# Moving one block's row gather behind the activation's turn in a routed expert loop

## The reference, cut to what matters

```python
def expert_block(args):
    xb, e = args
    return clamped_swiglu(xb @ w1[e] + b1[e]) @ w2[e] + b2[e]
yb = lax.map(expert_block, (xs, block_exp)).reshape(P, D)
y = jnp.zeros((T, D), h.dtype).at[row_tok].add(yb * row_gate[:, None])
```

## Time and profile before

| | us |
|---|---|
| time, median of 3 runs | 2306.31 (2303.6 to 2308.85) |
| span of the profiled execution | 2306.2 |
| TensorE busy | 2209.2 (96% of the span) |
| VectorE busy | 1194.8 (52%) |
| ScalarE busy | 650.0 (28%) |
| issues of weight chunks (BIG<-in_w, 1 MB each) | 384 |

### The profile page before, as it was taken

The page is one execution under the profiler, slowest core; times in us unless marked ns, Lnnn a source line. Parts: engine busy times, 40 slices in busy tenths (PEclk is TensorE's granted clock), DMA queues, the critical chain, the costliest instruction groups (busy, mean ns, idle before and its releaser), DMA issues. The chain is left out here.

```text
span 2306.2 us, 29645 instructions
## 1 busy us (share of the span) xinstructions
PE 2209.2 (96%) x10363; PEld 1188.4 (52%) x10364; DVE 1194.8 (52%) x2716; ACT 650.0 (28%) x1658; POOL 101.8 (4%) x234
## 2 busy tenths in 40 slices
PE   8999899999999999999999899999999999999997
PEld 3546685478744578777878633333333323333332
DVE  4989468453895563636745453334343333334334
ACT  3018442443221363336333321111111111111112
POOL 0001000000000051002001000000000000000000
PEclk9999999999999999999999999999999999999999
DMA  9670035301477103331241599989989998998998
GB/s 398 250 291 34 1 146 191 110 1 45 175 266 278 39 2 110 110 110 38 74 147 37 231 373 421 421 357 421 422 365 422 421 421 366 421 421 366 421 421 335
DMA packets 110280, 569.68 MB, mean 247 GB/s; under 512 B 11857, under 2 KB 13649, under 8 KB 51441
## 3 DMA queue, kind: packets, MB, share of 16 engines
q1 hardware_dynamic: 110192, 568.54, 61.6%
HBM read 567.46 MB, written 1.05 MB: 247 GB/s over the span
## 5 line engine op out<-in xcount | busy, mean ns | idle before, releaser
L3060 PE MATMUL PS<-BIG,PW 128*64 128x512 f32 x2304 | 514.1, 594 | 15.3 <-DMA BIG<-in_w 14.7
L3060 PEld LDWEIGHTS PS<-BIG,PW 128*64 128x64 f32 x2304 | 161.6, 137 | 353.6 <-issue 301.9
L3312 DVE TENSOR_SCALAR PW<-PS 128x512 f32<-128x512 f32 x36 | 24.9, 692 | 494.6 <-PE PS L3060 494.6
L3108 PE MATMUL PS<-BIG,PW 128*64 128x512 f32 x1152 | 255.4, 595 | 8.6 <-ACT PW L2923 8.6
L386 DVE SCALAR_TENSOR_TENSOR BIG<-BIG,COND_ROWS 128x1024 f32<-128x1024 f32 x128 | 153.4, 1221 | 24.9 <-DMA BIG<-in_w_ada_columns 24.6
L3108 PEld LDWEIGHTS PS<-BIG,PW 128*64 128x64 f32 x1152 | 79.2, 137 | 161.0 <-issue 142.7
L2900 ACT COPY BIG<-PS 128x512 f32<-128x512 f32 x37 | 21.7, 586 | 486.6 <-PE PS L3032 486.6
L1148 PE MATMUL PS<-HT,BIG 128*128 128x512 f32 (+1 forms) x448 | 152.0, 501 | 0.0
L1148 PEld LDWEIGHTS PS<-HT,BIG 128*128 128x128 f32 x448 | 85.1, 190 | 65.3 <-issue 60.3
L658 PE MATMUL PS<-HT,BIG 128*128 128x256 f32 x512 | 111.6, 379 | 1.4 <-PEq L863 1.4
L1553 PE MATMUL PS<-BIG,HT 128*128 128x512 f32 x256 | 110.0, 592 | 0.0
(11 more groups left out here) (547 smaller groups left out, 3171.6 us busy)
## 6 DMA issues: line engine op xcount, KB each, us to landing
BIG<-in_w SPq DMA_DIRECT2D x384, 1024.0 KB, 16.1
BIG<-in_l_w_ada_columns SPq DMA_DIRECT2D x40, 1024.0 KB, 7.2
BIG<-in_l_w_in SPq DMA_DIRECT2D x19, 2048.0 KB, 8.5
BIG<-in_w_ada_columns SPq DMA_DIRECT2D x24, 1024.0 KB, 7.1
BIG<-in_l_w_out SPq DMA_DIRECT2D x8, 2048.0 KB, 8.5
BIG<-in_w_in SPq DMA_DIRECT2D x7, 2048.0 KB, 8.1
BIG<-in_l_w_ada SPq DMA_DIRECT2D x4, 2048.0 KB, 17.9
BIG<-in_w_out SPq DMA_DIRECT2D x2, 2048.0 KB, 7.8
```

The lines of the kernel that those rows point to most:

```text
L3060: ins = nc.tensor.matmul(PS[64 * g:64 * g + 64, 4 + half, :], xt[:, c % 4, c // 4, :], W[:, c, half * F + g * 512:half * F + g * 512 + 512 ...
L3108: ins = nc.tensor.matmul(PS[64 * g:64 * g + 64, 7, :], at_[:, k % 4, k // 4, :], W[:, 8 + k // 2, k % 2 * D + g * 512:k % 2 * D + g * 512 ...
```

## The change

The gather of the rows of block i+1 goes from the middle of `first_products(i)` to `second_products(i)`, right behind the four turns of the activation. The turns of the gathered rows go from before the second products to behind the second of the eight pairs of second products (k == 2, so between chunk 8 and chunk 9). Block 0 keeps its old order (`gather_here=False`). On ScalarE the copy of the turned activation comes ahead of the copy of the gathered rows. The instructions themselves are the same ones, and as many. The diff, cut to its core:

```diff
                     def copies(i):
                         act.wait_ge(loop["act_turned"], i + 1)
                         nc.scalar.copy(at_, PS[:, 7, :].rearrange("p (j g s) -> p j g s", j=4, g=2)).then_inc(loop["act_copied"], 1)
-                        copy_turned(i + 1)
...
                     with act.Fori(1, n) as i:
-                        copy_gathered(i + 1)
                         sigmoid(i)
                         copies(i)
+                        copy_gathered(i + 1)
+                        copy_turned(i + 1)
...
-                    def products_and_gather(i, load):
-                        def gather_between(c):
-                            if c == 3:
-                                gather_next(i)
-
-                        first_products(i, load, beside=gather_between)
...
-                    def second_products(i, load, beside=None):
+                    def second_products(i, load, beside=None, gather_here=True):
                         pe.wait_ge(loop["act_ready"], i + 1)
...
                         ins.then_inc(loop["act_turned"], 1)
-                        turn_gathered(i + 1)
+                        if gather_here:
+                            gather_next(i)
+                        else:
+                            turn_gathered(i + 1)
                         pe.wait_ge(loop["act_copied"], i + 1)
                         for k in range(KT):
+                            if gather_here and k == 2:
+                                turn_gathered(i + 1)
...
-                        products_and_gather(i, load)
+                        first_products(i, load)
                         scatter_last(i)
                         second_products(i, load)
```

More of the change, by code:

```diff
@@ L2931, in _ @@
                     copies(0)
+                    copy_turned(1)
                     with act.Fori(1, n) as i:
-                        copy_gathered(i + 1)
                         sigmoid(i)
                         copies(i)
+                        copy_gathered(i + 1)
+                        copy_turned(i + 1)
                     def square_half(bank):
@@ L3146, in spread_gates @@
                         spread_places(1)
-                    second_products(0, 0, beside=spread_gates)
+                    second_products(0, 0, beside=spread_gates, gather_here=False)
                     load = pe.value_load(plan[0:1, 1:2], min_val=0, max_val=E - 1)
-                    products_and_gather(1, load)
+                    first_products(1, load)
                     scatter_last(1)
@@ L3155, in _ @@
                     load = pe.value_load(plan[0:1, 2:3], min_val=0, max_val=E - 1)
-                    products_and_gather(2, load)
+                    first_products(2, load)
                     pe.wait_ge(loop["bias2_scaled"], 1)
```

## The result

The changed kernel takes 2314.7 us (median of five runs, 2313.2 to 2315.8), the kernel before 2307.9 us beside it. The medians differ by 6.8 us. The ratio is 1.0035, 95% interval 1.0022 to 1.0047: by it the change is slower by 8.1 us, between 5.1 and 10.8. The forecast was 2314.3 us and +8.0.

What follows compares the result with a forecast made beforehand. The prediction took weight transfers and TensorE's five legs after chunk 7 to bound the kernel in turn. Each leg: +1.71 - 0.84 + 0.73 = +1.60 us; five add 8.0, giving 2314.3 us, range 2309.5 to 2319.5.

Steps and rivals of the forecast that it cites:

- The bound: Experts' stage: weight transfers (29.8 us a one-load block) are slower than TensorE's 26.07 us block; both limits take turns.
- the relay: Experts' stage: span 2306.2 us splits into 1505.1 ahead, 57.9 TensorE legs, 720.3 transfers and 22.9 ending.
- the legs: TensorE's path from chunk 7 to the next issue, 14.47 us four times, plus the ending; each forecast +1.60 us.
- the first stretch: Transfers ahead of the first of five waits for chunk 7: counted 0, up to 0.5 us gain kept for the range.
- The gather leaves the first products: Between chunks 3 and 4: removing its 1.71 us only lengthens TensorE's wait at chunk 7, worth 0.
- the steady block: TensorE's regular block from turn to turn, 26.07 us; forecast to fall by 0.11 us, spent waiting at chunk 7.
- The turns between chunks 8 and 9: Gathered rows' four transposes within the second products: +0.73 us on a leg, ScalarE's copy hidden with 1.1 us to spare.
- The sum: Per leg +1.71 - 0.84 + 0.73 = +1.60 us; five legs +8.0 us, median 2314.3 us.
- the transfers' stretches: From an issue to the next chunk 7, four times, 720.30 us together; forecast unchanged within some tenths.
- TensorE isn't the bound: Denies the rival that TensorE bounds the stage and the copy's stall counts: 2297.2 or 2302.5 us, chance 0.08.
- the gather isn't hidden on any leg: Denies the rival that the gather on the leg is hidden: time as before, 2306.3 us, chance 0.13.
- ScalarE's copy isn't late: Denies the rival that the gathered rows' copy is late at k == 2: 0.63 us a block, 2320.2 us, chance 0.07.

Runs made afterwards that it cites:

- the same kernel with a wait of 0.4: Kernel before with scatter moved behind chunk 3, gather behind chunk 7, and ScalarE's sigmoid ahead of the gathered rows' copy: 2310.2 us, ratio 1.0008.
- the kernel that waited 0.82 us a block: Kernel before with only the gather moved from behind chunk 3 to behind chunk 7, ScalarE's order as before: 2322.1 us, ratio 1.0061.

## Why the prediction was right, step by step

*The bound* was read rightly. Before and after, the relay's parts add up to the span, the legs come out to 0.01 us four times over, and two experiments say it from both sides: with half the transfers the order costs nothing in a block, and 60 us less work on TensorE are worth about 10. The pause of the DMA engines is 1.7 us longer on each leg, 1.6 forecast. One reading under it does not hold: a DMA share near 1 does not by itself say that the rate can't rise, nor do 377 GB/s say that the engines were not full, for the share beside the 377 is 0.99. The 0.5 us kept for the first stretch rested on that; the stretch came out 1.1 us shorter, in part by chance, as shown above.

*The gather leaves the first products: worth 0.* Right: the changed kernel waits for chunks 3 to 7 in the block where it had waited for 1 to 3, 6 and 7, and meets chunk 7 when it lands.

*The leg: +1.60 us forecast, +1.71 measured.* The term that was too small is the step from the activation's turns to the gather. I counted 0.57 us for four transposes and 1.71 for the gather; the rows show 1506.66 - 1505.98 = 0.68 and 1508.43 - 1506.66 = 1.77. The way back from 128-column transposes to 64-column products costs about 0.1 us here, where block 0 had shown nothing; behind the late turns it shows nothing again (1510.83 - 1510.24 = 0.59 for four). The Trainium skill, TensorEngine Tiling (Array Packing), Key Properties, says that changing the tiling mode drains TensorE, without telling one way from the other; the estimate by it was 1.75 us a leg, nearer to the 1.71 than mine, though only one of the two ways back shows a cost here. Because of the dearer steps the steady block stayed at 26.07 us instead of falling to 25.96.

*The turns between chunks 8 and 9*: 1510.83 - 1508.43 = 2.40 us from the products ahead of them to those behind, less 1.72 for the products themselves: 0.68 us, 0.73 forecast. ScalarE's copy was ready 1.0 us ahead of them (1.1 forecast), and `xt` kept nobody waiting.

*The sum*: 8.0 us forecast, 8.2 in the trace from the first issue on, 8.1 by the ratio with an interval of 5.1 to 10.8, 6.8 in the medians. That it comes nearer than its terms is luck: the five legs cost 8.5, and the first stretch (-1.1) and the transfers' stretches (+0.7) gave 0.4 back. That 2314.3 and 2314.7 us lie so close is luck too, since the kernel before took 2307.9 us beside the changed one and not 2306.3. The rivals fall. TensorE isn't the bound; the gather isn't hidden on any leg; ScalarE's copy isn't late. Not foreseen was how far the part ahead of the experts moves from run to run: the first issue for expert 1 lies between 1323.3 and 1330.2 us in these traces, with the same code ahead of it. That is nearly the size of the whole effect.

No experiment that still computes everything beats the kernel before by more than its interval. In the old order the leg may have little left to give: in the trace of before the weight load for chunk 11, at 1515.37 us, is released by that chunk's landing, without a pause beyond the usual 0.29 us, so that a shorter leg would have to wait there. That was not tried.

## What to carry to other kernels

Where two limits take turns, cut the span at the hand-overs and count a change only on the legs that it lies on; a stall that is removed from each of 36 blocks is worth nothing if a slower resource is waited for afterwards, and 1.7 us of work moved from ahead of that wait to behind it are paid in full, once per hand-over. Filling a short wait with longer work is a loss if the work came from the shadow of a longer wait. When a step is moved, look at what stands behind it in the program of every engine that waits for it: the same gather, moved with ScalarE's old order, cost more than twice as much, and with the scatter moved too some 115 us instead of next to nothing. And when one part of a time differs between two runs, measure the stretch from run to run ahead of the change before giving it a cause.

## What the hardware showed that was not expected

- The DMA share doesn't tell the rate: 0.99 goes with 377 GB/s and 1.01 with 422.
- Going from 128-column transposes to 64-column products cost about 0.1 us at one place (0.68 us against 0.57 for four transposes) and nothing at another (0.59).
- Behind a wait of 2.7 us in each block TensorE's granted clock fell to 1.2 GHz (second products 8.78 us instead of 7.09), so that the block was about 4.0 us longer than in the same kernel with a wait of 0.4 (30.4 and 26.4); in the kernel that waited 0.82 us a block the second products stayed at 7.09 us.
